# State-space stage: projections in another order, Y2 in the first norm's buffer, bias tables sent row by row

## What is computed

```python
zxbcdt = rms_norm(x, ln_g) @ in_w                 # z: 2048 columns, xbc: 3072, dt: 32
xbc = silu(causal_dwconv(xbc, conv_w, conv_b))    # four taps along the tokens
y = ssd_chunked(xs * dt, a, bm, cm)               # 4 groups of 8 heads, chunks of 128 tokens
y = (y + xs * d_skip) * silu(z)
y = rms_norm(y.reshape(b, s, 4, 512), norm_g)     # one norm for each group of 512 features
return y @ out_w
```

## Time and profile before

| | us |
|---|---|
| median of 3 runs (lowest, highest) | 2527.35 (2525.3, 2529.01) |
| the profiled execution's own time | 2528.55 |
| its span, first to last instruction | 2526.8 |
| TensorE busy | 2455.5 |
| VectorE, ScalarE, GpSimd busy | 1402.0, 977.4, 408.1 |
| mean granted TensorE clock | 0.987 of full |

### The profile page before, as it was taken

How to read it: one execution, slowest core, us unless ns; L and a number is a source line. 1 busy time by engine, 2 the same in 40 slices (tenths; PEclk the granted TensorE clock), 3 DMA queues, 4 the chain that set the end, 5 groups by cost and what they waited for, 6 DMA issues and landing times.

```text
span 2526.8 us, 30595 instructions
## 1 busy us (share of the span) xinstructions
PE 2455.5 (97%) x12080; PEld 1995.7 (79%) x12080; DVE 1402.0 (55%) x2273; ACT 977.4 (39%) x1597; POOL 408.1 (16%) x323
## 2 busy tenths in 40 slices
PE   7899999999999999999999999999999999999997
PEld 5677777888888888778888887787787887888886
DVE  6777776664566344656636546634554445443343
ACT  4333433442345344544324434423433334322222
POOL 0241423210121221222101110001200201110012
PEclk9999999999999999999999999999999999999998
DMA  4542122223323212113232232231134322223322
GB/s 147 92 92 71 63 83 68 96 95 94 101 87 104 88 63 68 51 59 101 91 108 93 87 123 84 63 113 59 55 94 136 117 93 92 92 94 99 101 85 80
DMA packets 73150, 226.24 MB, mean 90 GB/s; under 512 B 7728, under 2 KB 10928, under 8 KB 72880
## 3 DMA queue, kind: packets, MB, share of 16 engines
q1 hardware_dynamic: 66816, 212.01, 26.0%
q10 hardware_dynamic: 6192, 12.29, 2.4%
HBM read 215.87 MB, written 8.39 MB: 89 GB/s over the span
## 4 chain that ended last, share of the span: by engine, by line
PE 56%; DVE 1%; DMA 1%; ACT 1%; issue 1%; POOL 0%; DVEq 0%; POOLq 0%
PE bank L1102 55%; PE bank L1106 1%; DVE t L1891 0%; DMA t<-spill 0%; ACT t L1455 0%; POOL t L2451 0%; DMA t<-in_mem 0%; ACT t L1458 0%; DVE t L1894 0%; DVEq L2669 0%; DVE t L1902 0%; DVE t L2381 0%; POOL t L2454 0%; DVE t L1898 0%; DVE t L2222 0%
## 5 line engine op out<-in xcount | busy, mean ns | idle before, releaser
L1102 PE MATMUL bank<-t 128*128 128x512 f32 (+5 forms) x11736 | 2435.0, 373 | 55.4 <-DVE t L1891 27.1
L1102 PEld LDWEIGHTS bank<-t 128*128 128x128 f32 (+2 forms) x11736 | 1959.9, 187 | 501.4 <-issue 117.8
L1455 ACT ACTIVATE t<-t 128x1024 fp32r<-128x1024 f32 (+5 forms) x638 | 545.9, 867 | 675.7 <-PE bank L1102 277.9
L1891 DVE TENSOR_TENSOR t<-t 128x1024 fp32r<-128x1024 f32 (+5 forms) x682 | 626.6, 929 | 253.5 <-ACT t L1455 248.0
L2451 POOL TENSOR_TENSOR t<-t 128x512 f32<-128x512 f32 (+5 forms) x243 | 369.1, 1525 | 1678.0 <-ACT t L1458 571.5
L1891 DVE TENSOR_TENSOR t<-bank,t 128x512 f32<-128x512 f32 (+5 forms) x408 | 274.0, 676 | 523.7 <-PE bank L1102 483.2
L1458 ACT ACTIVATE t<-t 128x512 f32<-128x512 f32 (+5 forms) x553 | 335.0, 615 | 572.4 <-DVE t L1891 354.9
L1894 DVE SCALAR_TENSOR_TENSOR t<-t 128x512 f32<-128x512 f32 (+4 forms) x454 | 338.6, 753 | 127.6 <-ACT t L1455 63.6
L1455 ACT ACTIVATE t<-bank 128x512 f32<-128x512 f32 (+4 forms) x167 | 81.6, 505 | 187.0 <-PE bank L1102 111.7
L2454 POOL TENSOR_SCALAR t<-t 128x128 f32<-128x128 f32 (+3 forms) x64 | 38.4, 605 | 432.3 <-ACT t L1455 254.9
L1902 DVE CUSTOM_DVE_ANT_0 t<-bank,t 128x256 f32<-128x256 f32 (+3 forms) x128 | 55.6, 462 | 15.7 <-PE bank L1102 15.0
(11 more groups left out here) (24 smaller groups left out, 61.1 us busy)
## 6 DMA issues: line engine op xcount, KB each, us to landing
t<-in_w SPq DMA_DIRECT2D x314, 512.0 KB, 3.4
t<-in_w SPq DMA_DIRECT2D x48, 384.0 KB, 3.0
t<-in_w SPq DMA_DIRECT2D x48, 320.0 KB, 2.9
t<-in_w SPq DMA_DIRECT2D x24, 256.0 KB, 2.8
tab<-t ACTq DMA_DIRECT2D x1, 2560.0 KB
t<-in_x SPq DMA_DIRECT2D x8, 256.0 KB, 6.4
t<-tab SPq DMA_DIRECT2D x8, 256.0 KB, 4.0
spill<-t ACTq DMA_DIRECT2D x1, 2048.0 KB, 8.5
```

The costliest lines, as they stand in the source:

```text
L1102: return eng.matmul(out, lhs, rhs, start=start, stop=stop, skip_group_check=loose)
L1455: return eng.activation(out, in_, ACT.Copy, scale=scale)
L1891: return eng.tensor_tensor(out, a, b, o)
```

## The change

- Order: `group_z(3)` goes ahead of `out(1)`.
- `group_in(g)` for g of 2 and 3 waits in two steps: B and C only for the last pair of group g-2 and six ticks, the blocks of xs for `yn(g-2)` with no further tick, where all six waited for `yn(g-2)` and five ticks.
- Y2 goes to blocks 4 to 7 of `XAh` and `XAl`, so `yn(2)` waits for `group_z(3)` and no longer for `out(1)`.
- `rms` of groups 1 and 2 comes 11 ticks after `gate`, not 8. `sta(0)` comes two ticks later.
- Tables: 16 DMAs of one row each. Those of the first table are issued at ticks 36, 39, ... 57, those of the second at 60, 62, ... 74, where the two whole DMAs stood at 36 and 42. `yn(0)` may come 48 ticks after `tabs` (tick 78), not 14. All readers wait for 8 completions of each table.

```diff
-            self.once("sta", g, lambda g=g: have([("in", g, 0), ("in", g, 1)], 2)
+            self.once("sta", g, lambda g=g: have([("in", g, 0), ("in", g, 1)], 2 if g else 4)
...
-                if self.past("gate", g, 8) and self.when("rms", ("g", g)) is None:
+                if self.past("gate", g, 8 if g in (0, 3) else 11) and self.when("rms", ("g", g)) is None:
...
                 if g == 0:
-                    return self.past("tabs", 0, 14)
-                if g < 3:
-                    return ("out", g - 1, 7) in self.end
+                    return self.past("tabs", 0, 48)
+                if g == 1:
+                    return ("out", 0, 7) in self.end
                 return ("z", 3, 3) in self.end
...
-            if g >= 2:
-                self.until(lambda: self.past("yn", g - 2, 5), ("in", g))
             for i in range(6):
+                if g >= 2:
+                    before, age = (("pair", (g - 2, 3)), 6) if i < 2 else (("yn", g - 2), 0)
+                    self.until(lambda: self.past(*before, age), ("in", g, i))
...
         group_in(3)
+        group_z(3)
         out(1)
-        group_z(3)
         out(2)
...
+        elif src == "Y2":
+            return self.XAh[:, 4 + i, :], self.XAl[:, 4 + i, :]
...
-        for i, (name, ln) in enumerate((("tab1", L1), ("tab2", L2))):
-            for _ in at("tabs", T - 6 - 6 * i):
-                w.wait_ge(*empty(("tb", 2 * i + 1)))
-                eng.dma_start(dram[name], buf.tabs[i][:, 0:ln].unsqueeze(1).to_broadcast([8, P, ln])).then_inc(
-                    *sig.tabs[i].up())
+        for i, (name, ln, t0, step) in enumerate((("tab1", L1, 6, 3), ("tab2", L2, 30, 2))):
+            for h in range(8):
+                for _ in at("tabs", T - t0 - step * h):
+                    w.wait_ge(*empty(("tb", 2 * i + 1)))
+                    row = buf.tabs[i][h:h + 1, 0:ln].unsqueeze(1).to_broadcast([1, P, ln])
+                    eng.dma_start(dram[name][h:h + 1], row).then_inc(*sig.tabs[i].up())
...
                 if g == 0:
-                    w.wait_ge(*sig.tabs[0].at())
-                    w.wait_ge(*sig.tabs[1].at())
-                elif g < 3:
-                    w.wait_ge(*full(("out", g - 1, 7)))
+                    w.wait_ge(*sig.tabs[0].at(8))
+                    w.wait_ge(*sig.tabs[1].at(8))
+                elif g == 1:
+                    w.wait_ge(*full(("out", 0, 7)))
```

## The result

The changed kernel takes 2554.24 us (median of 4 runs, 2553.13 to 2556.23); the kernel before, run beside it, 2528.18. The ratio is 1.0105, with a 95% interval of 1.0089 to 1.0121: slower by 26 us. The forecast was 2565, within 2534 to 2610.

What follows compares the result with a forecast made beforehand. TensorE, busy 2455.5 of 2526.8 us, was taken as the bound. Waiting for slow rows (54) plus weights (7) less 23.2 won gave +38 on the median 2527.35: 2565 us, range 2534 to 2610.

Steps and rivals of the forecast that it cites:

- R1: Table DMAs: rows go at 50 GB/s or more, last row done by 160 us; 2504 us; chance 0.13.
- R2: Table DMAs: a row gets one DMA engine or one partition's eighth, 6.2 GB/s; kernel 3066 us; chance 0.01.
- R4: Whole change: order gains nothing, ScalarE's issues cost what is won, rows fit; 2522 to 2530 us; chance 0.03.
- R3: ScalarE's new issues are held, row behind row, and ticks follow the rows; 2578 us; chance 0.83 together with the forecast.
- (a): State-space start, sta(0) two ticks later: 2.37 us wait and 1.5 us of half-clock cost go; 3.9 us won.
- 54 for the wait: ScalarE's wait for the tables at tick 88: TensorE goes on at 251.6 us, 54 us late.
- 7 for weights: Weight loads queued behind table pieces slow the projections from tick 54 on: 7 us lost, between 0 and 20.
- (b): Second table's held issue: without it the 8.74 us stall and 2.7 us at half clock go; 11.4 us won.
- (c): Ticks 86 to 115, later rms and no empty ticks: 8.2 us less 4.4 for VectorE as the longer; 3.8 won.
- (d): group_z(3) ahead of out(1), Y2 in the other buffer: 3.46 us stall and 1.6 at half clock go; 5.1 won.
- a full queue: ScalarE's table issues: the ring being full would show as issues of over 5 us.

Runs made afterwards that it cites:

- spread tables: Changed order, tables made on 128 partitions and sent by two whole DMAs of 8 copies per partition, against the kernel before: 2506.10 us, 0.9912.
- four-apart tables: Changed order, two whole table DMAs, the 8 rows on partitions 0, 4, ... 28 instead of 0 to 7, against the kernel before: 2507.96 us, 0.9919.
- the second table late: Kernel before, second whole table sent at age 30 ticks instead of 12 and yn(0) from age 48: 2515.23 us, 0.9947.
- the last kernel: Changed order with tables sent from 128 partitions, but out(1) again ahead of group_z(3), Y2 still over n1, against the kernel before: 2516.42 us, 0.9950.

## Why the prediction was right, and where it wasn't

**The side and the cause.** A row is one source partition, so it runs at about half of what eight neighbours gave: 25 GB/s was taken, half of the 50 of the earlier trace rows; 27 was measured in a stretch, 29 over all. The tables needed 145 us instead of 168, and were out at 214, not at 242. The spread and the four-apart tables show that it is the source and which partitions it lies on. R1 and R2 fall with it: sixteen DMA engines on one row gave 27 GB/s, less than the 50 of the whole table and more than R2's 6.2, and R1's end of the tables (160 us) is 54 us off. R4 falls by the whole tables in the new order, which win 9 us.

**The place was R3's, not the forecast's.** The prediction let ScalarE stand once, 59 us at its wait for the tables at tick 88. That wait bound nothing: ScalarE came there at about 230 us, and the tables had been done for some 15. The step that failed is "they start at 73.5, one row queued behind the other without a gap": the queue doesn't take as many rows, so it is the issues that stop ScalarE, one after the other. (The rows did go out without a gap, from 70.2 us on; the 73.5 leaves out the 3 us that the sum itself wins by (a).) From the fourth on, issues were let go at the pace at which rows went out. The ends of the fourth to the tenth issue lie 11.5 to 12.6 us apart, with 0.328 MB at 27 GB/s being 12.1, and those of the last six 4.5 to 7.5, with 0.197 MB being 7.3. The ninth and tenth, held 12.06 and 12.08 us, already send rows of the second table: a hold is at most about as long as the row takes that goes out ahead. The ticks follow the rows, and the time is lost in seven stalls between 104 and 203 us. The prediction had this case as R3, at 2578.

**The size.** Rows cost 2554.2 - 2506.1 = 48 us, where 54 for the wait and 7 for weights had been put: 61. Two errors hide in the difference of 13, and they work against each other. With the measured 145 us in place of 168 the prediction's own path gives a wait that is 23 to 24 us shorter, 30 instead of 54, and a time of about 2541. The measured price is 48, some 11 us more than these 30 and 7. The runs don't split these 11, but the sum has no term for what the seven stalls do to the clock, and of the 45.5 us that the rows cost between ticks 42 and 86, 12.7 are slower work. So the side and the cause were right by their reasons, and the nearness of 2565 to 2554 is in part luck: a rate taken too low made up for a path that was too cheap. The 7 for weights showed only where GpSimd issued the rows; in the changed kernel no stall of ScalarE was put down to a load.

**The gains** were 23.2 in the sum and 22.1 in the kernel with spread tables (2528.2 - 2506.1), but not in their terms:
- (b), the held issue: 11.4 expected, 15 with spread tables in the old order and 13 with the second table late. From tick 42 to the end of `z(1)` the kernel before takes 111.6 us, and 99.0 with spread tables in its order. Fourteen more issues cost nothing as issues: sent far apart, 16 of them took 0.57 us or less each.
- (a): 3.9 expected, 3.1 between the two profiles, 1.2 between the two kernels with spread tables (the same matmul starts at 56.09 and at 54.87). The 2.37 us of stall are 0.50 to 0.52, as said; the rest differs from execution to execution, and in this stretch the kernel before and its version with spread tables, alike so far, differ by 1.4 us.
- (c): 3.8 expected, 3.3 measured, 4.9 with spread tables at full clock, and its stated cause half wrong. The three ticks of `rms` gave nothing. What is left is that the empty ticks are gone; that was not undone alone. VectorE is not the longer of the two there. With the clock at 1.00, in the kernel with spread tables, TensorE works 36.27 us of the stretch and VectorE 36.09, and the stalls are 0.97 and 1.86 us:

```profile
183.20:222.30 39.10, 36.27 (x173) 30.05 (x172) 36.09 (x46) 19.09 (x27) 5.36 (x4) 1.00 0.25 79
```

- (d): 5.1 expected, 2.3 measured. The hand count had Y3 cut as `out(3)` begins. It still came 1.22 and 0.84 us late, so of 3.46 us of stall 1.4 went. The 10 us of the last kernel are no part of this: they are what the new buffer costs without the new order.

**What was to be seen.** ScalarE idle 40 to 90 us at one copy near 185 us: wrong. TensorE idle in pieces from 110 us on: right, from 104, though by held issues and not by weights. The queue at 0.25 MB in 10 us: right (0.27), until 214 and not past 225. Weights landing in 20 us or more: right (23.7). No issue of 11 us: wrong, and the line said what it would mean, a full queue. No stall of over 1 us: right at `sta(0)` (0.52), wrong at the sums of group 1 (1.86) and at `out(3)` (1.22).

**What stays open.** What the queue counts isn't known. A whole table of 1024 pieces went in with 1.27 us, and the fourth row, behind 384 pieces of which some had gone, was already held; the second whole table was held 11.5 us and let go long before the first was out. It isn't a fixed number of pieces: when the second whole table was let in, 448 of the first's 1024 pieces had started and 576 were to come; when the fifth row was let in, 158 of the 512 before it were to come. Why 128 bytes cost TensorE 2% in the feed-forward stage was only measured.

## What to carry to other kernels

A broadcast DMA reads its few source partitions over and over, and neighbours share one way out: spread the source over partitions (or place its rows four apart) before cutting the DMA into smaller ones. If ScalarE's queue is fed faster than it drains, ScalarE stands at its issue for as long as a DMA ahead takes to go out, and everything in its program behind it; spacing issues by the time that one takes removes that even where the transfer stays slow. Before undoing one part of a reordering, look for the buffer that it was moved for: here the old order with the new buffer cost 10 us.

## What the runs showed of the hardware that wasn't expected

- The rate out of SBUF by source: one partition 27 GB/s (a piece of 2560 bytes 1.3 us with 16 DMA engines on it), partitions 0 to 7 50 GB/s, partitions 0, 4, ... 28 151 GB/s, all 128 140 GB/s.
- Held issues on ScalarE are let go at the pace of the queue: about 12 us apart while rows of 0.328 MB go out, 4.5 to 7.5 for 0.197 MB, 4 for 0.197 MB sent from eight rows. GpSimd's issues of the same rows were never held (0.75 us at most), and then loads on another queue took up to 62 us, with ScalarE's issues up to 33, and 3.4 without the tables.
- Tiles moved by 128 bytes in each partition: 174 matmuls in 40 us instead of 178 at a granted clock of 1.00, and 16 us of the whole program.
- Two rows in transit from different groups of four partitions go side by side: 0.33 MB in 8 us from 182 us on, where one row moves 0.21.
